# A hybrid decoder trunk on one core: constant products at four norms, row maxima and first mLSTM tiles drawn forward

## The reference

```
h = RMSNorm(x) * (1 + scale1) + shift1
x = x + gate1 * W_out [ NSA attention (8 heads x 64) | mLSTM (4 heads x 128) ]   # one input projection
h = RMSNorm(x) * (1 + scale2) + shift2
x = x + gate2 * (silu(conv3(h W_a)) * (h W_v)) W_down                             # 2816 hidden channels
```

## Time and profile before

| | |
|---|---|
| time, median of 3 runs | 1547.76 us (1542.69 to 1548.22) |
| the profiled execution | 1547.0 us, its span 1545.2 us |
| busy, PE / weight loads | 1466.0 us (95%) / 1198.3 us (78%) |
| busy, VectorE / ScalarE / GpSimd | 612.2 / 513.6 / 623.8 us |
| the chain that ended last | TensorE 79%, issue 8%, VectorE 4%, ScalarE 4% |
| mean granted clock | 0.970 of full speed |

### The profile page before, as it was taken

The page is one execution under the profiler, slowest core; times in us unless marked ns, Lnnn a source line. Parts: engine busy times, 40 slices in busy tenths (PEclk is TensorE's granted clock), DMA queues, the critical chain, the costliest instruction groups (busy, mean ns, idle before and its releaser), DMA issues.

```text
span 1545.2 us, 17840 instructions
## 1 busy us (share of the span) xinstructions
PE 1466.0 (95%) x7230; PEld 1198.3 (78%) x7230; DVE 612.2 (40%) x1056; ACT 513.6 (33%) x679; POOL 623.8 (40%) x284
## 2 busy tenths in 40 slices
PE   4899999989899999999989999999889999999997
PEld 4688876767688888878867888677768888887886
DVE  5736255558444454343130454474614221211002
ACT  4313334542243333221132234344514333332112
POOL 0533223113555454455533432322065555555461
PEclk8899999999999999999989999999999999999998
DMA  9632110035165666564332321100022333313321
GB/s 353 186 98 83 55 55 28 1 122 179 55 188 173 194 181 182 153 227 153 103 109 58 114 78 55 55 1 1 28 82 74 91 109 83 109 55 126 99 76 55
DMA packets 185047, 163.21 MB, mean 106 GB/s; under 512 B 16037, under 2 KB 151685, under 8 KB 184965
## 3 DMA queue, kind: packets, MB, share of 16 engines
q1 hardware_dynamic: 183796, 161.83, 34.1%
q10 hardware_dynamic: 1169, 0.25, 0.1%
HBM read 159.96 MB, written 2.10 MB: 105 GB/s over the span
## 4 chain that ended last, share of the span: by engine, by line
PE 79%; issue 8%; DVE 4%; ACT 4%; POOL 2%; DMA 1%; POOLq 1%; DVEq 0%; ACTq 0%; SPq 0%
PE psum L1474 18%; PE psum L1476 18%; PE psum L1475 18%; PE psum L1506 4%; PE psum L1507 4%; PE psum L1509 3%; PE psum L1778 2%; ACT w_hi L679 1%; POOL w_lo L539 1%; PE psum L1515 1%; PE psum L1619 1%; PE psum L1450 1%; PE psum L1641 1%; DVE psum L1002 1%; PE psum L1462 1%
## 5 line engine op out<-in xcount | busy, mean ns | idle before, releaser
L539 POOL TENSOR_TENSOR w_lo<-w_raw,w_hi 128x2048 fp32r<-128x2048 f32 x72 | 332.6, 4619 | 432.7 <-ACT w_hi L679 431.8
L679 ACT ACTIVATE w_hi<-w_raw 128x2048 fp32r<-128x2048 f32 (+2 forms) x104 | 192.8, 1854 | 639.6 <-PE psum L1476 458.6
L1474 PE MATMUL psum<-h_hi,w_hi 128*128 128x512 f32 x928 | 367.7, 396 | 2.8 <-POOL w_lo L539 1.9
L1476 PE MATMUL psum<-h_hi,w_lo 128*128 128x512 f32 x928 | 362.2, 390 | 0.0
L1475 PE MATMUL psum<-h_lo,w_hi 128*128 128x512 f32 x928 | 361.9, 390 | 0.0
L1474 PEld LDWEIGHTS psum<-h_hi,w_hi 128*128 128x128 f32 x928 | 174.8, 188 | 39.8 <-POOL w_lo L539 2.7
L1476 PEld LDWEIGHTS psum<-h_hi,w_lo 128*128 128x128 f32 x928 | 174.5, 188 | 37.3
L1475 PEld LDWEIGHTS psum<-h_lo,w_hi 128*128 128x128 f32 x928 | 174.8, 188 | 34.8
L555 POOL TENSOR_TENSOR w_lo<-w_raw,w_hi 128x1792 fp32r<-128x1792 f32 (+2 forms) x28 | 112.5, 4018 | 152.2 <-ACT w_hi L679 152.2
L1384 DVE SCALAR_TENSOR_TENSOR fy<-psum,par,fy 128x511 f32<-128x511 f32 x44 | 33.0, 750 | 289.5 <-ACT fy L876 289.5
L1474 PE MATMUL psum<-hid_hi,w_hi 128*128 128x512 f32 x352 | 140.1, 398 | 1.6 <-POOL w_lo L555 1.6
(11 more groups left out here) (261 smaller groups left out, 1945.5 us busy)
## 6 DMA issues: line engine op xcount, KB each, us to landing
w_raw<-in_ffn_up SPq DMA_DIRECT2D x88, 512.0 KB, 5.2
a_raw<-in_ada_w SPq DMA_DIRECT2D x56, 512.0 KB, 4.7
w_raw<-in_w_in SPq DMA_DIRECT2D x48, 512.0 KB, 4.6
w_raw<-in_ffn_down SPq DMA_DIRECT2D x32, 512.0 KB, 4.5
w_raw<-in_w_out SPq DMA_DIRECT2D x16, 512.0 KB, 4.4
a_raw<-in_ada_w SPq DMA_DIRECT2D x6, 1024.0 KB, 7.6
a_tok<-in_ada_w SPq DMA_DIRECT2D x6, 1024.0 KB, 8.0
w_raw<-in_ffn_down SPq DMA_DIRECT2D x16, 384.0 KB, 3.1
```

Source lines behind the costliest of these rows:

```text
L539: g.tensor_tensor(w_lo[:, slot_of(u), :], w_raw[:, slot_of(u), :], w_hi[:, u % HI, :].bitcast(F32), ALU.subtract).then_inc(s_lo, 1)
L679: s.activation(w_hi[:, u % HI, 0:n], w_raw[:, r, 0:n], ACT.Copy).then_inc(s_hi, 1)
L1474: m(ps, l_hi, r_hi, start=first, stop=False)
L1476: return m(ps, l_lo, r_hi, start=False, stop=last)
```

## The change

1. Every `last_unit` gets a spare bank. Behind its products TensorE runs six bf16 products of constants (`keep_clock`: identity times the triangular mask, 512 columns, into the spare bank), then the last square sums, six more, the spread, and (except at the final norm) six more. The spread moves into `last_unit` from behind it. The wait ahead of the last unit asks for more residual updates, as the spare bank must be read: 6 instead of 2 at the output projection, 4 instead of 2 at the down projection.
2. The low queries of blocks 0 and 1 get a tile of their own, `qe`, over the second half of `pt`. ScalarE copies them and their maxima rows ahead of its wait for unit 13. TensorE issues `max_rows(0)` and `(1)` at step 6 of unit 13. In it now run maxima 0 to 11 (3, 3, 3, 2, 1 at steps 3 to 7); 12 to 15 run between the first two score steps.
3. The gate columns move from behind values 18 to behind scores 19, ScalarE's copies of them from behind the last exponential to behind exponential 18, and VectorE's `gate_scan` from z = 14 to z = 13. mLSTM tiles 0 and 1 are computed ahead of values 18 and 19, tile 0 in banks 6 and 7; the others take the pairs (1, 0, 2) in turn. Tile 0 waits for `s_acol`, tile 3 for the last `gated`.

```diff
+        qe = place("qe", [P, 2, R, P], F32R, at=late + 4096)
+        def low_q(b):
+            return qe[:, b] if b < 2 else block_q(qm, b)
+        def mix_pair(z):
+            return pair(3 if z == 0 else (1, 0, 2)[(z - 1) % 3])
...
 # ScalarE
+                    if u == U_OUT - 1:
+                        for b in range(2):
+                            s.activation(low_q(b), block_q(qk, b).bitcast(F32), ACT.Copy)
+                        act.drain()
+                        max_rows(0)
+                        max_rows(1)
                     if u >= U_MQK:
                         unit_used(act, l, u)
-                        if u == U_OUT - 1:
-                            for b in range(2):
-                                s.activation(block_q(qm, b), block_q(qk, b).bitcast(F32), ACT.Copy)
...
-                act.drain()
-                max_rows(0)
-                max_rows(1)
...
-                act.wait_ge(s_col, l + 1)
...
+                    if z == NZ - 2:
+                        act.wait_ge(s_col, l + 1)
+                        cols = bank[6][:, 0:2 * TT * MH].rearrange("p (i t h) -> p i t h", i=2, t=TT)
+                        s.activation(acol[:, 0], cols[:, 0], ACT.Copy)
+                        s.activation(acol[:, 1], cols[:, 1], ACT.Exp, scale=-1.0).then_inc(s_acol, 1)
+                        act.drain()
...
 # VectorE
-                    if z == 14:
+                    if z == 13:
                         gate_scan()
...
 # TensorE
+            def keep_clock(n, b):
+                for _ in range(n):
+                    m(bank[b].rearrange("p (a q) -> p a q", a=TT), identb[:],
+                      triT[:].unsqueeze(1).broadcast_to([P, TT, P]), start=True, stop=True)
...
-            def last_unit(u, banks, nk, rhs, first, n):
+            def last_unit(u, banks, nk, rhs, first, n, spare):
...
+                keep_clock(6, spare)
                 sum_squares(n, (2,))
+                keep_clock(6, spare)
+                spread(n)
+                if n < 2 * L:
+                    keep_clock(6, spare)
...
-                        for n in range(3 * kk - 9, 3 * kk - 6) if kk >= 3 else ():
+                        if kk == 6:
+                            max_rows(0)
+                            max_rows(1)
+                        for n in ((), (), (), (0, 1, 2), (3, 4, 5), (6, 7, 8), (9, 10), (11,))[kk]:
                             maxima(n)
...
-                maxima(WHOLE - 1)
-                max_rows(0)
-                max_rows(1)
...
                 key_scores(0)
+                for n in range(12, WHOLE):
+                    maxima(n)
                 key_scores(1)
...
+                    if z >= NZ - 2:
+                        sources(z - NZ + 2)
                     values(z)
...
-                    if z == NZ - 2:
+                    if z == NZ - 3:
                         gate_columns()
...
+                    if z == 0:
+                        pe.wait_ge(s_cv3, l * 2 * MH + 2 * MH)
+                        pe.wait_ge(s_acol, l + 1)
+                    elif z == 3:
+                        pe.wait_ge(s_gated, l * NBLK + NBLK)
+                    elif z > 3:
+                        pe.wait_ge(s_mWS, l * 16 + z - 2)
...
-                        pe.wait_ge(s_xu, KD + 2 * KD * l + 2)
+                        pe.wait_ge(s_xu, KD + 2 * KD * l + 6)
...
-                            pe.wait_ge(s_xu, 2 * KD + 2 * KD * l + 2)
+                            pe.wait_ge(s_xu, 2 * KD + 2 * KD * l + 4)
```

More of the change, by code:

```diff
@@ L742, in sigmoids, with max_rows @@
                     s.activation(gat[:], gif[:, :, 0:NGATE], ACT.Sigmoid).then_inc(s_gat, 1)
+                def max_rows(b):
+                    act.wait_ge(s_nr, l * NBLK + b + 1)
+                    if b >= 2:
+                        act.wait_ge(s_qm, l * (NBLK - 2) + b - 1)
+                    rows = bank[4 + b if b < 2 else 2 * (FIRST[b] % 2)][DH:DH + 2 * R, 0:P]
+                    for h in range(R):
+                        last = s.activation(low_q(b)[DH:DH + 2 * R, h, :], rows, ACT.Copy,
+                                            scale=own[DH:DH + 2 * R, h:h + 1])
+                    last.then_inc(s_nrow, 1)
                 for u in range(U_OUT):
@@ L842, in _ @@
                                 act.wait_ge(s_mWS, l * 16 + z - 2)
-                            s.activation(mw[:, z % 3, 0:n], pair(z % 3)[1][:, 0:n], ACT.Exp,
+                            s.activation(mw[:, z % 3, 0:n], mix_pair(z)[1][:, 0:n], ACT.Exp,
                                          bias=acol[:, 0, j, h:h + 1]).then_inc(s_mW, 1)
@@ L1339, in _ @@
                         v.scalar_tensor_tensor(out=mws[:, h % 2, W_OFF[j]:W_OFF[j] + n],
-                                               in0=pair(z % 3)[0][:, 0:n], scalar=MSCALE, in1=mw[:, z % 3, 0:n],
+                                               in0=mix_pair(z)[0][:, 0:n], scalar=MSCALE, in1=mw[:, z % 3, 0:n],
                                                op0=ALU.mult, op1=ALU.mult).then_inc(s_mWS, 1)
@@ L1572, in _ @@
             for l in range(L):
-                if l:
-                    spread(2 * l)
                 ada_at_step = {(1, 3): 4, (2, 1): 5, (U_OUT + 1, 1): 6, (U_OUT + 1, 6): 7, (U_OUT + 2, 3): 8,
@@ L1763, in key_scores @@
                         m(ps, qk[:, J_K + 2 * br + gr, keys], block_q(qk, b), start=True, stop=False)
-                        last = m(ps, qk[:, J_X + 2 * br + gr, keys], block_q(qm, b), start=False, stop=kb < t)
+                        last = m(ps, qk[:, J_X + 2 * br + gr, keys], low_q(b), start=False, stop=kb < t)
                         if kb == t:
@@ L1781, in values, with sources @@
                     last.then_inc(s_PV, 1)
+                def sources(z):
+                    h, j = z // TT, z % TT
+                    n = (TT - j) * P
+                    if z == 0:
[5 more added lines that the diff above has]
+                        pe.wait_ge(s_mWS, l * 16 + z - 2)
+                    ps, bc = mix_pair(z)
+                    m(ps[:, 0:n], mqk[:, MH + h, j * P:(j + 1) * P], mqk[:, h, j * P:T], start=True, stop=True)
+                    m(bc[:, 0:n], pick[:, h:h + 1].broadcast_to([P, P]), arow[:, j * P:T], start=True, stop=False)
+                    m(bc[:, 0:P], identb[:], triT[:], start=False, stop=True).then_inc(s_mS, 1)
                 pe.wait_ge(s_vone, l + 1)
                 key_scores(0)
+                for n in range(12, WHOLE):
+                    maxima(n)
                 key_scores(1)
@@ L1822, in head_values @@
                             last.then_inc(s_mO, 1)
[L1824 to L1828, removed]
+                for z in range(2, MH * TT):
                     sources(z)
@@ L1859, in _ @@
                     if q == 3:
-                        last_unit(u, pair((q + 2) % 3), KD, h_of, True, 2 * l + 1)
+                        last_unit(u, pair((q + 2) % 3), KD, h_of, True, 2 * l + 1, 2)
                     else:
                         column_unit(u, pair((q + 2) % 3), KD, h_of, True, True, mixed if q == 0 else None, beside_ada(u))
-                spread(2 * l + 1)
                 def up(l, f):
@@ L1912, in _ @@
                     if u == UNITS - 1:
-                        last_unit(u, pair((q + 1) % 3), k1 - k0, hidden, False, 2 * l + 2)
+                        last_unit(u, pair((q + 1) % 3), k1 - k0, hidden, False, 2 * l + 2, 4)
                     else:
@@ L1916, in _ @@
                                     made if q == 0 else None)
-            spread(2 * L)
             for c8 in range(KD):
```

## The result

The changed kernel takes 1537.5 us (median of 12 runs, 1528.2 to 1539.0), the kernel before 1547.4 (12 runs, 1541.4 to 1552.4): a ratio of 0.9924, 95% interval 0.9903 to 0.9945, so 10 us faster where the sum of the forecast had 14. The mean granted clock rose from 0.970 to 0.983. First the head of the page of the changed kernel; the row `PEclk` gives the clock in tenths for 40 slices of the span.

What follows compares the result with a forecast made beforehand. TensorE was taken as the bound, with idle time at seams and stretches at 1.2 GHz to win. Terms -10.1 + 2.5 - 8.2 + 2.0 = -13.8 from 1547.0 gave 1533.2, stated as 1534 us; range 1528 to 1544.

Steps and rivals of the forecast that it cites:

- likeliest case: The whole forecast, all four parts as priced: 1534 us, own range 1530 to 1538, chance 0.60.
- Part 1: Constant products at the four norms fill TensorE's waits and keep its clock up: 10.1 us saved.
- Clock 1.0 through the norms, spreads of about 1.0: Sign of being right, at the norms: full granted clock, spreads about 1.0 us, no slow records behind them.
- The rival that the clock falls all the same: At the norms, constants fail to hold the clock: 6.7 us lost, none of 10.1 gained, 1550 us; chance 0.10.
- two records follow them: First up unit after norm 3: two records after VectorE's last low chunks, ending 1169.6, so 2.3 us saved.
- VectorE's chunks: Low chunks behind the norms: no faster clock speeds them, limiting norm 3 to 2.3 us and norm 1 to 1.7.
- Part 2: Last output unit of each layer waits for six updates, not two: stalls 0.85 and 1.6, 2.5 us lost.
- second rival: New stalls drop the clock behind last-unit waits and in seams to the mLSTM; four more give 1540; chance 0.17.
- Part 3: Attention's start: row maxima written while the last mLSTM unit runs, 4.1 us saved a layer, 8.2 in sum.
- the rival of ScalarE's lateness: Attention's start: late row copies lose 2 us a layer, 1538; chance 0.13 shared with norms half kept.
- Part 4: Seam from attention to mLSTM: gate columns and first score tiles earlier, last scores to tile 4 11.15; 2.0 us lost.
- a stretch at 1.2 GHz here again, 1.5 a layer: Seam to the mLSTM: thin gate columns, a wait and 65-column values drop TensorE's clock, costing 1.5 us a layer.

Runs made afterwards that it cites:

- rows_only: The kernel before with only the row maxima at attention's start moved; no constant products, old waits, old order at attention's end: 1537.2 us, ratio 0.9924.
- nt_zero: The changed kernel with the old order of gate columns and mLSTM tiles, and without the 66 constant products: 1540.7 us, ratio 0.9958.
- nt_gates: The changed kernel with the old order of mLSTM tiles and the gate columns four steps ahead of their old place: 1528.7 us, ratio 0.9877.
- gates_const2: As gates_const, but three constant products behind each of the two groups of gate columns, not four behind both: 1526.1 us, ratio 0.9865.
- gates_spare0: nt_gates with the output projection's constant products in a bank read one unit earlier, four updates awaited instead of six: 1527.2 us, ratio 0.9858.
- gates_const: gates_spare0 with four constant products behind both groups of gate columns: 1525.5 us, ratio 0.9855.

## Why the prediction was right, and where it was off

The sign, the range and the mechanism held: 1537.5 in a range of 1528 to 1544, at the upper end of the likeliest case's own range (1530 to 1538).

- **Part 1, mechanism right.** "Six cost 1.4": 1.46. "Clock 1.0 through the norms, spreads of about 1.0": 1.00 and 1.13. Norm 2 gave 4.6 where 4.7 were forecast, but that close a match is partly luck: the stage took 22.9 us in the profile of the kernel before, and only 20.7 and 20.6 in rows_only and nt_zero, which have no constants there either and whose clock came back earlier. Against those two the constants gave 2.4 and 2.3. That the constants and not the moved spread do it is shown by nt_zero. The rival that the clock falls all the same is refuted.
- **Part 1, a size off.** Norms 1 and 3 gave 0.7 and 1.3, not 1.7 and 2.3. The step that was mis-sized is "two records follow them" behind VectorE's last low chunk. VectorE and TensorE at norm 3 of the changed kernel:

```profile
1161.53 1.78 DVE L980 SCALAR_TENSOR_TENSOR h_lo<-hm,mod,h_hi 128x512 fp32r<-128x512 f32 x2
```

```profile
1162.70 0.73 PE L1900 MATMUL psum<-h_lo,w_hi 128*128 128x512 f32 x2
...
1164.65 0.39 PE L1488 MATMUL psum<-h_hi,w_hi 128*128 128x512 f32 x1
```

  The last low chunk ended at 1163.31, but TensorE left the unit at 1164.65. It had waited for the chunk before it, and from 1162.70 eight records were still to be done, 1.95 us. The bound was VectorE's, as said, but at chunk 6 and not 7: about 1.0 a norm. Norm 4 gave 1.8 instead of 1.4.
- **VectorE's chunks** did not get faster with TensorE's clock (second line: GpSimd's four quarters behind norm 1):

```profile
L980 DVE SCALAR_TENSOR_TENSOR h_lo<-hm,mod,h_hi x32: 739/935/1341, 46.4 to 1162.6; 128x512 fp32r<-128x512 f32 x32
411.34 6.39 POOL L556 TENSOR_TENSOR w_lo<-w_raw,w_hi 128x512 fp32r<-128x512 f32 x4 [14.72 <-ACT w_hi L688]
```

  Shortest, median and longest are those of the earlier trace rows, the longest even 13 ns more. The bound that the forecast took from this held. The Trainium skill (SBUF — State Buffer, "Who interferes with whom") has a VectorE instruction with two SBUF inputs and a GpSimd instruction that reads SBUF shut each other out for a whole instruction. The trace agrees in the direction and not in the extent: the four quarters ran from 411.34 to 417.73, and three whole low chunks of VectorE (1.27, 1.12, 1.12) within them. At their shortest times that is 4 x 1.28 + 3 x 0.74 = 7.3 us of work in 6.4, so the two overlapped.
- **Part 2** cost 0.81 and 1.60 (0.85 and 1.6 forecast), in the waits. No slow stretch followed them, against that part of the second rival.
- **Part 3** gave 4.3 a layer where 4.1 were forecast. ScalarE's rows ended at 232.1, half a microsecond later than forecast, and still ahead of the first scores; the rival of ScalarE's lateness did not come.
- **Part 4 is the term that was mis-sized.** Its structure was right: 11.15 us worked out for full clock, 11.0 measured in layer 0, with the waits foreseen (0.44 for the gate columns, 0.63 for the combine, 0.77 at tile 4; 0.7 or more was said of the last two). In layer 1, where the clock was down, the waits were 0.44, none, and 0.35. The term of the sum for this part was 2.0 lost; it measured 4.0. It put "a stretch at 1.2 GHz here again, 1.5 a layer". In the profile the stretch came in one layer and cost 3.9 to tile 4 and more behind: layer 0 won 1.3 and layer 1 lost 5.3. The stretch of part 3 was taken as the pattern, in which dense scores follow the wait; here values of 65 columns and small tiles follow, and the clock stayed down for 17 us. That the thin work behind it is why it lasted is argued from this, not tested. The second rival, new stalls that drop the clock elsewhere, is true at this place alone. Its 1540 was nearer in the median than the forecast's sum of 1533.
- **What the baseline had.** The forecast set the new order at full clock, 11.15, against seams that were themselves slow (12.4 and 10.8, clock 0.72 and 0.84 in the earlier trace rows), and so found 1.3 won and 0.35 lost. At the same clock the old order needs about 9.0 by nt_gates (7.1 and 1.9 for the gate columns, an estimate), so the new one costs some 2 a layer. The slow stretches of the seam could be taken away without it, as gates_const2 shows.

The runs of the changed kernel lie in two groups: two at 1528.2 with a mean granted clock of 0.992, eight at 1537.1 to 1539.0 with 0.982 to 0.985, two between. (0.992 - 0.983) x 1536 is 14 us of lost full clock, 28 us at the lower level; the profiled run is one of the second group (0.983), and its stretch of some 17 us would be most of that. So the 10 us between the groups go with slow stretches; that they are this very seam isn't shown, as only one execution was profiled. Open as well are which part of the thin work decides whether a seam falls for 6.8 or for 17 us, and whether gates_const2 is better than gates_spare0.

## What to carry to other kernels

When the work in front of a wait is thin, products of constants into a free bank, sized to the wait, can keep TensorE's clock at next to no cost: here 66 of them gave 8 to 9 us. They did so where they came before the clock fell (gates_const2) and not where they came behind (gates_const), and the bank must be one whose reader is done, or it adds its own wait. Compare a new order with the old one at the same clock, as a baseline with slow stretches flatters it. Of each new order write down how long its waits and its thin work are in a row, and work its stages out at both clock levels; a busy TensorE says nothing on that, the `PEclk` and the spacing of records do. Put tiny transposes where the engine waits anyway, and dense products between them.

## What the runs showed of the hardware that was not expected

- TensorE at 98% busy (16.84 of 17.2 us) can stay at 1.2 GHz for 17 us: here the records were products of 65 columns and small tiles; behind norm 2 of the kernel before, with dense unit work, it was back after 14 records, 6.1 us.
- The clock can fall with no wait close ahead of it: in nt_gates a slow stretch of 6.8 to 10.2 us begins at the end of two groups of 4-column products in both layers, with no recorded wait in the 6 us before them, and with three dense products behind each group it is gone (gates_const2). In layer 0 of the changed kernel it did not fall behind the same groups.
- VectorE and GpSimd slow each other down in part and not by whole instructions: a low chunk of 0.74 us took 1.12 to 1.27 beside GpSimd's quarters, and a quarter 1.56 where the shortest took 1.28.
- The time of a run goes with its mean granted clock: gates_const ran in 1522.1 us at 0.991 and in 1530.7 at 0.985, the same kernel on the same chip.
